# Moving four modulation products of a two-layer diffusion trunk: two into the first mixer, three behind the first layer's experts

## The reference, cut to what matters

```python
mod = jax.nn.silu(cond) @ P['ada_w'][l] + P['ada_b'][l]      # ada_w[l] is 1024 x 6144
sh1, sc1, g1, sh2, sc2, g2 = jnp.split(mod[:, None, :], 6, axis=-1)
h = x * (1.0 + sc1) + sh1
out = even_mixer(h, ...) if l % 2 == 0 else hyena_mixer(h, ...)
x = layer_norm(ALPHA * x + g1 * out, ln_w[l, 0], ln_b[l, 0])
h = x * (1.0 + sc2) + sh2
y = moe_ffn(h, ...)                                          # 16 experts, top 2
x = layer_norm(ALPHA * x + g2 * y, ln_w[l, 1], ln_b[l, 1])
```

## Time and profile before

| | |
|---|---|
| three runs | 1298.92, 1307.53, 1307.13 us; median 1307.13 |
| profiled execution | 1303.92 us, of it 1302.2 us from the first to the last instruction |
| PE / DVE / ACT / POOL busy | 991.1 / 415.4 / 228.1 / 164.3 us |
| data moved by DMA | 345.06 MB, mean 265 GB/s |
| mean granted TensorE clock | 0.900 of full |

### The profile page before, as it was taken

How to read it: one execution, slowest core, us unless ns; L and a number is a source line. 1 busy time by engine, 2 the same in 40 slices (tenths; PEclk the granted TensorE clock), 3 DMA queues, 4 the chain that set the end, 5 groups by cost and what they waited for, 6 DMA issues and landing times.

```text
span 1302.2 us, 23736 instructions
## 1 busy us (share of the span) xinstructions
PE 991.1 (76%) x9370; PEld 553.3 (42%) x9370; DVE 415.4 (32%) x1135; ACT 228.1 (18%) x455; POOL 164.3 (13%) x323
## 2 busy tenths in 40 slices
PE   1899998698289759794489999898938997775830
PEld 0444446554245435352245554445424553332510
DVE  0220117855422212121453234553541221111207
ACT  0401002513212111121221111110321211110202
POOL 1200001100221111112020000001022111110121
PEclk9999999799689989898799998899958998887965
DMA  9995324577379999999994113633631969999973
GB/s 323 374 306 204 105 108 137 195 310 290 152 281 388 395 396 394 404 367 390 392 377 150 45 60 104 257 130 138 254 158 41 329 245 393 401 407 404 391 275 133
DMA packets 78858, 345.06 MB, mean 265 GB/s; under 512 B 8086, under 2 KB 8537, under 8 KB 66508
## 3 DMA queue, kind: packets, MB, share of 16 engines
q1 hardware_dynamic: 57108, 289.30, 57.6%
q0 software_dynamic: 13648, 43.84, 9.9%
q10 hardware_dynamic: 8040, 11.01, 2.5%
HBM read 320.50 MB, written 23.63 MB: 264 GB/s over the span
## 4 chain that ended last, share of the span: by engine, by line
PE 57%; DMA 23%; DVE 11%; ACT 3%; issue 2%; SPq 2%; POOL 1%; POOLq 0%; ACTq 0%; DVEq 0%; PEldq 0%
DMA ring<-in_moe_w_up_dram 15%; PE bank L830 15%; PE bank L636 11%; PE bank L895 10%; PE bank L759 6%; PE bank L837 6%; DMA ring<-in_ada_w_dram 5%; PE bank L589 2%; SPq L1323 2%; DMA ring<-in_moe_w_down_dram 1%; PE bank L969 1%; PE bank L993 1%; ACT arena L1181 1%; PE bank L907 1%; DVE arena L1292 1%
## 5 line engine op out<-in xcount | busy, mean ns | idle before, releaser
L830 PE MATMUL bank<-ring,arena 128*32 128x256 f32 x3072 | 193.9, 409 | 51.7 <-DMA ring<-in_moe_w_up_dram 49.5
L830 PEld LDWEIGHTS bank<-ring,arena 128*32 128x32 f32 x3072 | 105.0, 118 | 133.4 <-issue 76.1
L636 PE MATMUL bank<-ring,hT 128*128 128x512 f32 x336 | 144.9, 593 | 1.0 <-ACT hT L1029 1.0
L1290 DVE TENSOR_TENSOR arena<-arena,bank 128x64 f32<-128x64 f32 x136 | 27.4, 201 | 316.1 <-ACT arena L1181 316.1
L895 PE MATMUL bank<-hT,ring 128*128 128x384 f32 x384 | 124.6, 487 | 1.0 <-ACT hT L1029 1.0
L837 PE MATMUL bank<-ring,arena 128*32 128x256 f32 x1536 | 92.8, 382 | 27.5 <-DVE arena L1292 25.4
L589 PE MATMUL bank<-ring,small 128*32 128x256 f32 x768 | 55.5, 453 | 62.1 <-DMA ring<-in_ada_w_dram 62.1
L636 PEld LDWEIGHTS bank<-ring,hT 128*128 128x128 f32 x336 | 63.6, 190 | 80.6 <-issue 79.3
L895 PEld LDWEIGHTS bank<-hT,ring 128*128 128x128 f32 x384 | 72.7, 190 | 52.5 <-ACT hT L1029 1.2
L830 PE MATMUL bank<-arena 128*32 128x256 f32 x1216 | 74.3, 399 | 14.8 <-DMA arena<-in_moe_w_up_dram 14.8
L837 PEld LDWEIGHTS bank<-ring,arena 128*32 128x32 f32 x1536 | 45.1, 109 | 58.6 <-DVE arena L1292 31.9
(11 more groups left out here) (316 smaller groups left out, 1093.9 us busy)
## 6 DMA issues: line engine op xcount, KB each, us to landing
ring<-in_ada_w_dram SPq DMA_DIRECT2D x24, 2048.0 KB, 19.1
ring<-in_moe_w_gate_dram SPq DMA_DIRECT2D x22, 2048.0 KB, 22.0
ring<-in_moe_w_up_dram SPq DMA_DIRECT2D x22, 2048.0 KB, 27.0
ring<-in_moe_w_down_dram SPq DMA_DIRECT2D x22, 2048.0 KB, 29.9
arena<-in_moe_w_gate_dram SPq DMA_DIRECT2D x10, 2048.0 KB, 35.6
arena<-in_moe_w_up_dram SPq DMA_DIRECT2D x10, 2048.0 KB, 41.3
arena<-in_moe_w_down_dram SPq DMA_DIRECT2D x10, 2048.0 KB, 44.3
ring<-in_ev_w_in_dram SPq DMA_DIRECT2D x7, 2048.0 KB, 16.4
```

Source lines behind the costliest of these rows:

```text
L636: last = pe.matmul(bank[3 * (c % 2) + t], hT[:, k, t * P:(t + 1) * P], slot8(n)[:, k, :], start=k == 0, stop=k == KT - 1)
L830: last = pe.matmul(bank[1][q * BLK:(q + 1) * BLK, 0:HALF], slot_inT[:, k, :], both[:, :, k, q * P:(q + 1) * P], start=k == 0, stop=k == KT ...
L1290: dve.tensor_tensor(act_rows[:, two, :], silu_g[:, two, :], up, ALU.mult).then_inc(S["gated"], 1)
```

## The change

Pairs (1,0) and (1,1) are loaded and multiplied in the first mixer: (1,0) behind (0,2), (1,1) in the place of (0,5). Pair (0,5), the gate of LN, goes behind the experts, ahead of (1,2) and (1,3). ACT copies these three pairs one after the other at the head of `act_ln(1)`. POOL asks for LN's weight and bias rows where it did, then waits for pair (0,5) and writes its gate rows (`pool_gates(1)`), then does its waits and the six gathers, and only then reads the gate rows back (`ln_gate_rows`). DVE's wait for those rows stands behind its first instruction on tile 0. The ring's slots are numbered anew, and `modulation_due` replaces the counts that assumed the old order.

```diff
-ADA_ORDER = [(0, 0), (0, 1), (0, 3), (0, 2), (0, 4), (0, 5), (1, 0), (1, 1), (1, 2), (1, 3), (1, 4), (1, 5)]
+ADA_ORDER = [(0, 0), (0, 1), (0, 3), (0, 2), (1, 0), (0, 4), (1, 1), (0, 5), (1, 2), (1, 3), (1, 4), (1, 5)]
...
-          + pair_chunks(0, 2) + pair_chunks(0, 4) + pair_chunks(0, 5) + matrix_chunks("ev_out", 0, 2))
-BETWEEN = (pair_chunks(1, 0) + pair_chunks(1, 1) + pair_chunks(1, 2) + pair_chunks(1, 3) + matrix_chunks("hy_in", 0, 6)
+          + pair_chunks(0, 2) + pair_chunks(1, 0) + pair_chunks(0, 4) + pair_chunks(1, 1) + matrix_chunks("ev_out", 0, 2))
+BETWEEN = (pair_chunks(0, 5) + pair_chunks(1, 2) + pair_chunks(1, 3) + matrix_chunks("hy_in", 0, 6)
...
# pool_moe
-            ln_rows(pool, 2 * l + 1)
+            ln_weight_rows(pool, 2 * l + 1)
+            if l:
+                ln_gate_rows(pool, 2 * l + 1)
+            else:
+                pool_gates(pool, 1)
...
# pool_moe, behind the gathers
+            if l == 0:
+                ln_gate_rows(pool, 1)
...
# pe_mixer
             pe_ada(pe, 0, 2, bank[4])
+            pe.wait_ge(ret_dve, 1)
+            pe_ada(pe, 1, 0, bank[7])
...
             pe_ada(pe, 0, 4, bank[4])
-            pe_ada(pe, 0, 5, bank[3])
+            pe_ada(pe, 1, 1, bank[3])
...
+            pe_ada_columns(pe, 1, 0, bank[6])
             pe_ada_columns(pe, 0, 4, bank[7])
+            pe_ada_columns(pe, 1, 1, bank[5])
...
# act_ln
             if n == 1:
-                act_ada(act, 1, 0, bank[0])
+                act_ada(act, 0, 5, bank[2])
+                act_ada(act, 1, 2, bank[3])
+                act_ada(act, 1, 3, bank[7])
             for t in range(NT):
-                if n == 1 and t == 2:
-                    act_ada(act, 1, 1, bank[1])
                 act.wait_ge(gathered[t], 32 * (j + 1))
                 act.activation(ln_sum(n, t), ln_sum(n, t), ACT.Copy, scale=wsel[:, 0, t:t + 1]).then_inc(ln_first, 1)
...
-                    if n == 1:
-                        act_ada(act, 1, 2, bank[2])
-            if n == 1:
-                act_ada(act, 1, 3, bank[7])
...
# PE's program
             pe_moe(pe, 0, MOE0)
-            pe_ada(pe, 1, 0, bank[0])
-            pe_ada(pe, 1, 1, bank[1])
-            pe_ada_columns(pe, 1, 0, bank[0])
-            pe_ada(pe, 1, 2, bank[2])
-            pe_ada_columns(pe, 1, 1, bank[1])
+            pe_ada(pe, 0, 5, bank[2])
+            pe_ada(pe, 1, 2, bank[3])
             pe_ada(pe, 1, 3, bank[7])
             pe_ada_columns(pe, 1, 3, bank[7])
```

More of the change, by code:

```diff
@@ L77, in ring_slots @@
 def ring_slots():
-    slots = [(i + 4) % STAGING for i in range(len(BEFORE))] + [i % MOE_RING for i in range(3 * NE)]
-    slots += [(i + 3) % STAGING for i in range(len(BETWEEN) - 5)] + [0, 1, 2, 3, 4] + [i % MOE_RING for i in range(3 * NE)]
+    slots = [(i + 2) % STAGING for i in range(len(BEFORE))] + [i % MOE_RING for i in range(3 * NE)]
+    slots += [(i + 3) % STAGING for i in range(len(BETWEEN) - 6)] + [0, 1, 2, 0, 3, 4] + [i % MOE_RING for i in range(3 * NE)]
     seen = [0] * MOE_RING
@@ L469, in wait_counted, with ln_weight_rows, ln_gate_rows @@
             eng.reg_add(reg, reg, step)
-        def ln_rows(pool, n):
-            l, s = n // 2, n % 2
-            g = at(LN_ROWS, 2, D)
+        def ln_weight_rows(pool, n):
+            for k, name in enumerate(("ln_w", "ln_b")):
+                pool.dma_start(at(LN_ROWS + (2 + k) * D, D), a[name][n // 2, n % 2:n % 2 + 1, :].to_broadcast([P, D])).then_inc(lnrow_in, 16)
+        def ln_gate_rows(pool, n):
             pool.wait_ge(gate_out[n], 64)
             for group in range(2):
-                pool.dma_start(g[:, group, :], gates[l, s, group:group + 1, :].to_broadcast([P, D])).then_inc(lnrow_in, 16)
-            pool.dma_start(at(LN_ROWS + 2 * D, D), a["ln_w"][l, s:s + 1, :].to_broadcast([P, D])).then_inc(lnrow_in, 16)
-            pool.dma_start(at(LN_ROWS + 3 * D, D), a["ln_b"][l, s:s + 1, :].to_broadcast([P, D])).then_inc(lnrow_in, 16)
+                pool.dma_start(at(LN_ROWS + group * D, D), gates[n // 2, n % 2, group:group + 1, :].to_broadcast([P, D])).then_inc(lnrow_in, 16)
         def tile_row(n, kind, half):
@@ L575, in act_ada, with modulation_due @@
             act.activation(mod_rows[q], b[:, 0:HALF], ACT.Copy).then_inc(mod_row, 1)
+        def modulation_due(m):
+            return 1 + max(COLUMN_PAIRS.index((m // 2, 3 * (m % 2) + i)) for i in range(2))
         def pe_condition(pe):
@@ L743, in pe_mixer @@
                 if k == 3:
-                    pe.wait_ge(mod_row, ADA_ORDER.index((0, 5)) + 1)
+                    pe.wait_ge(mod_row, ADA_ORDER.index((1, 1)) + 1)
                 for t in range(NT):
@@ L1024, in act_modulate @@
             scale, shift = mod_cols(m)
-            act.wait_ge(modT_rdy, 2 * (m + 1))
+            act.wait_ge(modT_rdy, modulation_due(m))
             for k in range(0, KT, 2):
@@ L1033, in dve_modulate @@
             scale, shift = mod_cols(m)
-            dve.wait_ge(modT_rdy, 2 * (m + 1))
+            dve.wait_ge(modT_rdy, modulation_due(m))
             for k in range(1, KT, 2):
@@ L1101, in total @@
                 link(dve.scalar_tensor_tensor(r, picked[:, t, 1, :], wsel[:, 1, t:t + 1], r, ALU.mult, ALU.add))
+                if t == 0:
+                    dve.wait_ge(lnrow_in, ROWS_DUE[n])
                 link(dve.tensor_tensor(r, r, gt, ALU.mult))
@@ L1106, in total @@
                 dve.bn_aggr(mv[:, t, :], stats[:, t, :]).then_inc(ln_var, 1)
-            dve.wait_ge(lnrow_in, ROWS_DUE[n])
             total(0)
@@ L1344, in load_moe @@
                         if SLOT[n] == STAGING:
-                            sp.wait_ge(modT_mm, 4 * (layer + 1))
-                            sp.wait_ge(gate_out[2 * layer], 64)
-                            sp.wait_ge(gate_out[2 * layer + 1], 64)
+                            sp.wait_ge(modT_mm, (COLUMN_PAIRS.index((1, 1)) + 1, len(COLUMN_PAIRS))[layer])
+                            for gate in ((0,), (1, 2, 3))[layer]:
+                                sp.wait_ge(gate_out[gate], 64)
                         elif SLOT[n] < STAGING:
@@ L1410, in gpsimd_program @@
             tile_rows(pool, 0)
-            pool_gates(pool, 1)
             pool.wait_ge(x_half, 2 * NT)
@@ L1534, in scalar_program @@
             act_ada(act, 0, 2, bank[4])
+            act_ada(act, 1, 0, bank[7])
             for u in range(12):
@@ L1546, in scalar_program @@
             act_ada(act, 0, 4, bank[4])
-            act_ada(act, 0, 5, bank[3])
+            act_ada(act, 1, 1, bank[3])
             for k in range(0, KT, 2):
@@ L1731, in vector_program @@
                 dve.tensor_copy(hT[:, k, :], bank[k][:, 0:T]).then_inc(cT_dve, 1)
+            dve_ada_columns(dve, 1, 0, bank[6])
             dve_ada_columns(dve, 0, 4, bank[7])
+            dve_ada_columns(dve, 1, 1, bank[5])
             dve_tiles(dve, link, 0)
@@ L1735, in vector_program @@
             dve_ln(dve, link, 1)
-            for q, b in ((0, 0), (1, 1), (3, 7)):
-                dve_ada_columns(dve, 1, q, bank[b])
+            dve_ada_columns(dve, 1, 3, bank[7])
             dve_modulate(dve, 2)
```

## The result

The changed kernel takes 1324.8 us (median of four runs, 1320.96 to 1326.24), the kernel before 1305.45 beside it. The ratio is 1.0152, with a 95% interval of 1.0108 to 1.0197: slower by about 20 us. The profiled execution has a span of 1319.2 us, 17.0 more than before.

What follows compares the result with a forecast made beforehand. Bytes bound the stretch behind the experts, PE the second layer after it. LN's delay 15.1, clock 1.7 and mixer 0.1 sum to +16.9 us: 1320.8 from the profiled execution, 1324.0 from the median; predicted 1322, range 1308 to 1330.

Steps and rivals of the forecast that it cites:

- What bounds the stage: Between experts and second layer's projection: bytes set the time, LN runs inside the weight stream with 4.2 us of slack.
- Bytes behind the experts: Behind the experts: three pairs instead of four, 10.7 us fewer bytes at 392 GB/s, third pair at 647.7 (644 to 650).
- LN: First layer's last LayerNorm: first scaling waits for the third copy (653.85), then 26.1 us; PE transposes x 15.1 us later.
- The clock: PE behind LN: coming back from an idle stretch at a lower granted clock costs 1.7 us (0 to 2.3).
- The first mixer: First mixer: pair (1,0) fits PE's idle 7.75 us, two added chunks cost nothing on DMA; in all +0.1 us.
- the columns' 0.6: First mixer: two more pairs of column transposes ahead of the output projection cost 0.6 us (0 to 0.8).
- the clock's 0.5: First mixer: less PE idle time may keep the granted clock up, a gain of 0.5 us (0 to 2.2).
- The sum: Shift of the second layer's projection start: 15.1 + 1.7 + 0.1 = +16.9 us, giving 1320.8 from the profiled execution.
- the step that each later stage takes as long as before: After the second layer's projection starts: PE bounds throughout, so the end moves by as much as that start.
- The rival "third pair before the gathers": Behind the experts: weights served before 8.0 us of gathered rows, third pair at 639.7, time 1313; chance 0.12.
- The rival "bytes alone count": Behind the experts: LN keeps its cover, the projection starts 10.7 us earlier, time 1293; chance 0.08.
- The rival "a second wait on top": LN also waits for late gate rows, or added mixer bytes hold up the output projection; 1326 to 1332; chance 0.06.

Runs made afterwards that it cites:

- copies_first: The kernel before with one edit: ACT copies all four pairs (1,0) to (1,3) ahead of LN's first scaling; ratio to the kernel before 1.0196.
- one_pair_moved: Against the changed kernel: only (1,0) moves into the first mixer, (0,5) stays there, ACT's copies and POOL's gate handling as before; ratio to the kernel before 0.9910.
- copies_late: The changed kernel with ACT's copies of (1,2) and (1,3) put back inside and behind LN; ratio to the kernel before 1.0055.
- gathers_first: The changed kernel with POOL issuing the six gathers ahead of its wait for pair (0,5) and the gate writes; ratio to the kernel before 1.0102.
- changed_again: The changed kernel unaltered, timed again; ratio to the kernel before 1.0133.
- copies_late_gathers_first: The changed kernel with ACT's copies of (1,2) and (1,3) put back and POOL's six gathers ahead of its gate wait; ratio to the kernel before 1.0014.

## Why the prediction was right, point by point

*What bounds the stage.* Right. copies_first and one_pair_moved show the two sides of it: order alone costs 25.9 us, a pair moved out is worth 11.3, both by the fourth column.

*Bytes behind the experts.* Right, though the third pair came to PE at 652.18, not 647.73, and so past my bound of 650: the whole stretch had begun late. The last down-projection started at 606.10 and not at 601.46, and behind it the pair came 46.1 us later, where I had 46.3 (647.73 - 601.46). So the row's rate of 392 GB/s held. The gathers left at 629.07, behind the pair's copy and the four gate writes, as the step on POOL's wait had it.

*LN.* Right, and exact: from the first scaling (659.15) to the last write of x (683.97 + 1.3) are 26.1 us, the figure from the earlier trace rows. copies_late shows that ACT's order is what delays it, gathers_first that POOL's order isn't while ACT's stands. What the prediction didn't see is how much would be left without the copies: with both orders undone the stage is still 4.8 us longer than before (72.6 against 67.8), because LN waits for the gate pair's way through DRAM.

*The clock.* Right in one profile, too large in the other. From the start of PE's main block of transposes to the projection are 5.07 us (685.31 to 690.38) and in changed_again 5.96 (from 681.96), before 4.24: +0.8 and +1.7, against my 1.7. A part of the clock's cost I had put at nothing: the third pair's own matmuls took 6.20 us (5.65 in changed_again) behind a wait of 14 to 15 us, where I had taken 5.35.

*The first mixer.* Pair (1,0) fitted the idle stretch: PE was idle 3.88 us where it had been idle 7.75. The clock gain that I had hoped for didn't come. The window of before in the earlier trace rows has its counterpart in

```profile
236.00:241.00 5.00, 3.62 (x21) 2.58 (x22) 3.41 (x15) 2.51 (x12) 2.07 (x4) 0.65 1.05 387
250.00:260.00 10.00, 8.30 (x65) 6.90 (x64) 9.12 (x28) 6.87 (x20) 0.00 (x0) 0.94 0.89 331
```

and though the clock is 0.65 there it was lower afterwards: from (0,2)'s first matmul to the output projection are 54.1 us (224.38 to 278.50) where they were 53.1 (222.34 to 275.45). In changed_again they are 53.1 (223.85 to 276.96). So the mixer's term is 0 to +1.0, in which my +0.1 lies; but no run tells its parts apart, the columns' 0.6 and the clock's 0.5. The added bytes are the 331 GB/s in a window that had 5, and nothing waited for them.

*The sum.* Counted from the last down-projection, where drifts of earlier stages don't count (us):

| | forecast | changed | changed_again |
|---|---|---|---|
| to the third pair's first matmul | 46.3 | 46.1 | 46.0 |
| to LN's first scaling | 6.1 | 7.0 | 6.4 |
| LN, to the end of the last write of x | 26.1 | 26.1 | 26.1 |
| to the projection | 6.1 | 5.1 | 6.0 |
| sum | 84.6 | 84.3 | 84.6 |

The stage took 67.8 us before, so this is +16.8 forecast (16.9 without the mixer's 0.1) and +16.5 and +16.8 measured. In the first profile of the changed kernel two misses, 0.9 us more to the first scaling and 1.0 less to the projection, cancel: that part of the closeness is luck.

Counted from the program's start the projection is 21.1 and 18.6 us late. Of this 2.0 and 1.5 were there before the retention's score matmuls (209.07 and 208.54 against 207.02). These don't come from the new slots: copies_first, which opens like the kernel before, has these matmuls at 210.18, and copies_late_gathers_first, which opens like the changed kernel, reaches pair (0,2) at 222.19, where before had 222.34. The rest is the mixer's 0 to 1.0 us and the experts' 0.5 to 1.3.

The end of the first profile moved by 17.0 us only, because 4.3 us were given back in the second mixer (221.4 us from projection to output projection, 225.7 before and in changed_again), see the last section; changed_again ends 20.2 later. So the step that each later stage takes as long as before, PE bounding it throughout, failed by 4.3 us in this execution. That its 1320.96 us lie beside my 1320.8 is luck: 4.6 us of lateness ahead of the last down-projection, and 4.3 given back in the second mixer. By the timed ratios, 1.0152 and 1.0133, the kernel lost 20 and 17 us.

*The rival "third pair before the gathers"* was wrong as the rows had it: the second pair came at 631.04, the third at 652.18, 21 us apart, with gathers and gate rows between them. *The rival "bytes alone count"* is refuted by copies_first, which loads nothing in addition and is 2% slower. *The rival "a second wait on top"* didn't come about: the gate rows, asked for at 636.32, were there when DVE first used them at 661.72, right behind its instruction before. In copies_late, where LN starts earlier, they are what DVE waits for.

## What to carry to other kernels

An instruction that only passes on a result for later use is a barrier for everything behind it on its engine: ask of each wait what is queued behind it, above all when several such copies are gathered at the head of a stage. In a stage bound by DMA, the other engines' serial work is free only while the stream runs, so removing bytes helps up to the point where that work is as late as the bytes (here one pair, some 11 us or 1% of the kernel), and anything that delays its start is paid in full. A result that needs a way through DRAM ahead of the next step (here the gate: waits of 6 to 10 us for its way out, and 10 to 16 us back, with the DMA queues full) should be made a stage earlier than one that doesn't.

## What the runs showed of the hardware that was not expected

A small write to DRAM and its read back took long while the DMA share stood at 1.04: in copies_late_gathers_first POOL waited 10.26 us for four 2 KB gate writes (6.43 in gathers_first), and 10.2 us passed from asking for the two 512 KB broadcast reads to DVE's use of them (15.6 in copies_late).

The same matmuls of the second mixer took different times in different executions, by the granted clock behind a stop of 2.5 us. Timeline of PE, the kernel before and then the changed kernel:

```profile
817.17 3.78 PE L989 MATMUL bank<-arena 128*128 128x512 f32 x4 [2.53 <-DVE arena L1784]
```

```profile
836.59 1.98 PE L1004 MATMUL bank<-arena 128*128 128x512 f32 x4 [2.54 <-DVE arena L1794]
```

and the windows that begin there, the kernel before and then the changed kernel:

```profile
818.00:822.00 4.00, 4.00 (x6) 1.64 (x5) 0.00 (x0) 1.37 (x2) 0.00 (x0) 0.50 1.06 390
```

```profile
837.00:841.00 4.00, 4.00 (x10) 1.63 (x9) 0.00 (x0) 1.86 (x3) 0.00 (x0) 1.00 1.06 392
```

After the same stop the clock had fallen to its lower level in one execution and not in the other; changed_again, the same program as the changed kernel, fell (3.78 us for the same four matmuls). Of the nine profiles six have 3.78 us there, copies_late_gathers_first 2.63, the changed kernel and copies_first 1.98. Behind this stop it makes 2.5 us of difference and over the whole stage 4.3, all of it in PE's busy time (211.3 us before, 207.0 in the changed kernel, 211.3 in changed_again), and no edit explains it.
